# Seven block products instead of eight in twelve chunks more per layer, and attention moved into two PSUM banks

## The chip, the core and the metric

One core of a Trainium2 chip runs the whole program in one launch. The metric is device time in microseconds. TensorE (PE) multiplies, VectorE (DVE) and ScalarE (ACT) prepare operands and take results, GpSimd (POOL) and SyncE (SP) issue transfers.

## The reference

Two layers on x of 256 x 2048, all in float32:

```
h = rmsnorm(x, norm_mix[l]);  proj = h @ w_in[l]
qa, ka, va, qi, ki, wi, qb, kb, vb = split(proj)
o_a = top-k attention: 8 heads of 128; an indexer (16 heads of 64) scores all keys, the best 64 per query stay
o_b = sliding-window attention: 16 query heads, 2 key heads of 64, window 128, a sink per head
g_a, g_b = split(sigmoid(h @ w_gate[l]))
x = x + (g_a * (o_a @ w_branch_a[l]) + g_b * (o_b @ w_branch_b[l])) @ w_out[l]
x = x + relu(rmsnorm(x, norm_mlp[l]) @ w_up[l])**2 @ w_down[l]
```

and a last rmsnorm. Everything is causal in chunks of 64 positions. The key, index-weight and kb/vb columns of w_in are a first unit of their own ("misc").

## The kernel before

Every large product is cut into units of 512 output columns, and a unit into chunks of 256 rows of the weight (512 KB each). A float32 product is made of three faster ones: both operands are split into a high and a low half, and hi x hi, hi x lo and lo x hi are added. For each chunk, SP loads it into one of four buffers `raw`, ScalarE rounds it into `w_hi` (its `split`, L922), VectorE subtracts for `w_lo` (its `split`, L1350), and TensorE runs 12 matmuls of 512 columns into the two banks of a pair `acc[0]` or `acc[1]`, which alternate by unit. All engines walk the same list of chunks in the same order, each in its own queue, with semaphores between them. ScalarE may fill a slot as soon as TensorE has finished the chunk four before (`SLOTS = 4`); SP may load a buffer once the low half four before is taken.

Some chunks are "wide": the 256 x 512 block and the matching 256 x 256 of h are seen as 2 x 2 blocks and multiplied with seven block products instead of eight (`seven_products`, L532, a Winograd form). For this VectorE adds weight blocks (`weight_sums`, L1353, run before the split of the chunk ahead), the split has 7 x 256 columns instead of 4 x 256 (L929, L931 on ACT, L1371 on DVE), sums of blocks of h must exist in high and low halves (`s_hh`), and at the unit's end results in two further banks, the "sides" `wide_acc`, are added in (`add_up_sides`, L1760). Before, wide chunks are in branch B's gates (`WIDE_GATE`, chunks 1, 3, 5, 7) and in the MLP.

A layer has the misc unit, ten projection units of 8 chunks (`C_WIN`: 0 and 1 the indexer's queries, 2 and 3 qa, 4 and 5 ka, 6 and 7 va, 8 and 9 qb), then four times a branch A gate (8 chunks) and a branch product (4 chunks) from `C_MIXA`, the same for B, the out projection and the MLP. Attention is fitted between these chunks by hand: `jobs_after` (one for each engine) runs a job after a given chunk; ScalarE and VectorE come to the same list four chunks later (`AHEAD`), that is, after the split of chunk c+4 they do the part that belongs to TensorE's chunk c. Visits:

- indexer rounds at `IDX_AT` = C_WIN + 24, every fourth chunk two rounds on TensorE, top-k from `TOPK_AT` = C_WIN + 40;
- branch A, a head every second chunk from `A_AT` = C_WIN + 56: TensorE does the product with v of the head three before (`a_pv`) and the logits (`a_logits`); VectorE bias and row minimum (`a_low`), ScalarE the exponential (`a_exp`, L1020), VectorE normalises and spreads, GpSimd's transfers transpose through DRAM, and ScalarE copies the landed probabilities to `probsT` (`a_take_probsT`, L1032), one head earlier than the head whose exponential it has just done: at visit h the exponential of h, then the copy of h-2, then, at TensorE's visit h+1, its product;
- branch B, two groups of heads every fourth chunk from `B_AT` = C_MIXA + 4, in the same manner (`b_pv` two visits after `b_logits`).

Logits go to `att[0]` and `att[1]`, products with v to `att[2]`. Projections are read out by ScalarE (`take_win`, L1128) before its fourth split of the next unit, spread by VectorE (`spread_block`), and passed through DRAM by SP (`pass_on`: a store before load 7 of the unit, four fetches behind it), then placed by ScalarE.

## Time and profile before

| | us |
|---|---|
| median of 3 runs (lowest, highest) | 2659.84 (2659.27, 2660.45) |
| profiled execution | 2658.03 |
| its span | 2656.1 |
| TensorE busy, granted clock | 2641.4, 0.999 of full |

The span runs from the first to the last instruction; the time of an execution has a little more around it. A matmul's length in the trace overlaps the next one's, so costs are read as the distance from start to start. Layer 0's projections run from about 28 to 267 us, branch A's gates to about 413, branch B's after them.

### The profile page before, as it was taken

The numbers are of one execution on the slowest core, as the hardware profiler recorded it, in microseconds if no ns is written. First come the engines' busy times: TensorE is split into PE (matmuls) and PEld (weight loads), VectorE is DVE, ScalarE is ACT, GpSimd is POOL, SyncE is SP. The second block draws the span as 40 slices with busy tenths as digits, with TensorE's granted clock in tenths as the row PEclk, the third lists the DMA queues.
The fourth block names the chain that finished last, engine by engine and source line by source line (L and its number), as shares of the span: only waits on it lengthen the run. The fifth ranks groups of instructions, "written<-read, shape, count | busy, mean of one in ns | idle before, by whom it ended". The sixth has DMA issues, their size and how long they took to land.

```text
span 2656.1 us, 37301 instructions
## 1 busy us (share of the span) xinstructions
PE 2641.4 (99%) x13432; PEld 2217.1 (83%) x13432; DVE 2078.8 (78%) x3099; ACT 1448.1 (55%) x1863; POOL 215.8 (8%) x378
## 2 busy tenths in 40 slices
PE   9999999999999999999999999999999999999998
PEld 7788778888888888888888887788888888888887
DVE  5667678967898897987756766789678989989875
ACT  5445555545565655655455455555456556556554
POOL 0103110000100100100010021100000001000000
PEclk9999999999999999999999999999999999999999
DMA  7877676666775766767777666667677767667574
GB/s 260 239 236 224 222 226 195 229 231 231 244 228 191 246 216 206 240 205 232 235 237 225 224 225 221 218 202 233 227 256 231 221 208 242 209 217 234 189 248 151
DMA packets 187395, 594.52 MB, mean 224 GB/s; under 512 B 25576, under 2 KB 46612, under 8 KB 187088
## 3 DMA queue, kind: packets, MB, share of 16 engines
q1 hardware_dynamic: 166256, 536.94, 62.1%
q0 software_dynamic: 20432, 54.86, 7.5%
q8 instruction: 106, 1.74, 0.3%
q14 instruction: 73, 0.60, 0.1%
q10 hardware_dynamic: 528, 0.37, 0.1%
HBM read 544.58 MB, written 47.48 MB: 223 GB/s over the span
## 4 chain that ended last, share of the span: by engine, by line
PE 95%; DVE 3%; DMA 1%; issue 1%; ACT 0%; DVEq 0%; POOLq 0%; POOL 0%; SPq 0%; ACTq 0%
PE acc L578 24%; PE acc L579 24%; PE acc L580 24%; PE att L546 2%; PE att L548 2%; PE att L547 2%; PE acc L546 2%; PE acc L548 2%; PE acc L547 2%; PE acc L595 1%; PE acc L594 1%; PE acc L596 1%; DMA raw<-in_w_main 1%; DVE w_lo L1350 1%; DVE w_lo L1371 1%
## 5 line engine op out<-in xcount | busy, mean ns | idle before, releaser
L1350 DVE TENSOR_TENSOR w_lo<-raw,w_hi 128x1024 fp32r<-128x1024 f32 (+1 forms) x778 | 933.2, 1211 | 374.0 <-ACT w_hi L922 370.3
L922 ACT ACTIVATE w_hi<-raw 128x1024 fp32r<-128x1024 f32 (+1 forms) x778 | 813.1, 1051 | 633.5 <-PE acc L580 462.4
L578 PE MATMUL acc<-w_hi,h_hl 128*128 128x512 f32 x1848 | 735.2, 398 | 1.1 <-DVE w_lo L1350 1.1
L580 PE MATMUL acc<-w_hi,h_hl 128*128 128x512 f32 x1848 | 728.9, 394 | 0.0
L579 PE MATMUL acc<-w_lo,h_hl 128*128 128x512 f32 x1848 | 728.6, 394 | 0.0
L578 PEld LDWEIGHTS acc<-w_hi,h_hl 128*128 128x128 f32 x1848 | 347.9, 188 | 83.0 <-issue 4.9
L580 PEld LDWEIGHTS acc<-w_hi,h_hl 128*128 128x128 f32 x1848 | 347.9, 188 | 81.3
L579 PEld LDWEIGHTS acc<-w_lo,h_hl 128*128 128x128 f32 x1848 | 348.2, 188 | 76.3
L1371 DVE TENSOR_TENSOR w_lo<-raw,w_hi 128x1792 fp32r<-128x1792 f32 x166 | 335.5, 2021 | 33.5 <-ACT w_hi L931 32.4
L578 PE MATMUL acc<-w_hi,o_hl 128*128 128x512 f32 x912 | 360.4, 395 | 0.0
L579 PE MATMUL acc<-w_lo,o_hl 128*128 128x512 f32 x912 | 360.0, 395 | 0.0
L580 PE MATMUL acc<-w_hi,o_hl 128*128 128x512 f32 x912 | 359.6, 394 | 0.0
L929 ACT ACTIVATE w_hi<-raw 128x768 fp32r<-128x768 f32 x166 | 140.3, 845 | 195.0 <-PE acc L548 110.1
L931 ACT ACTIVATE w_hi<-raw 128x1024 fp32r<-128x1024 f32 x166 | 174.9, 1054 | 86.9 <-DVE raw L1365 86.7
L580 PEld LDWEIGHTS acc<-w_hi,o_hl 128*128 128x128 f32 x912 | 171.8, 188 | 40.2
L578 PEld LDWEIGHTS acc<-w_hi,o_hl 128*128 128x128 f32 x912 | 171.6, 188 | 37.7 <-issue 1.4
L579 PEld LDWEIGHTS acc<-w_lo,o_hl 128*128 128x128 f32 x912 | 171.7, 188 | 36.3
L1359 DVE TENSOR_TENSOR raw<-raw 128x512 f32<-128x512 f32 x166 | 113.3, 683 | 21.2 <-issue 11.3
L455 POOL DMA_DIRECT2D scratch<-spread x30 | 16.9, 563 | 973.2 <-DVE spread L1428 973.2
L1428 DVE STREAM_TRANSPOSE spread<-stage 128x512 f32<-128x512 f32 x112 | 73.0, 689 | 21.8 <-ACT stage L1128 17.5
L1020 ACT ACTIVATE probs<-probs,low 128x128 f32<-128x128 f32 x96 | 41.0, 428 | 85.0 <-DVE sink_d L1592 43.8
L1363 DVE TENSOR_TENSOR raw<-raw 128x256 f32<-128x256 f32 x166 | 70.6, 425 | 5.8
(298 smaller groups left out, 3614.9 us busy)
## 6 DMA issues: line engine op xcount, KB each, us to landing
raw<-in_w_main SPq DMA_DIRECT2D x928, 512.0 KB, 4.3
scratch<-spread SPq DMA_DIRECT2D x37, 512.0 KB, 2.8
moved<-scratch SPq DMA_DIRECT2D x148, 128.0 KB, 3.2
scratch<-spread POOLq DMA_DIRECT2D x30, 512.0 KB, 3.5
moved<-scratch POOLq DMA_DIRECT2D x120, 128.0 KB, 5.0
scratch_p<-spread POOLq DMA_DIRECT2D x16, 384.0 KB, 4.6
moved<-scratch_p POOLq DMA_DIRECT2D x64, 96.0 KB, 4.3
raw<-in_w_misc SPq DMA_DIRECT2D x16, 336.0 KB, 4.0
```

The lines of the kernel that those rows point to most:

```text
L546: nc.tensor.matmul(o, a_hi, hi[:, w], start=start, stop=False, skip_group_check=True)
L547: nc.tensor.matmul(o, a_hi, lo[:, w], start=False, stop=False, skip_group_check=True)
L548: return nc.tensor.matmul(o, a_lo, hi[:, w], start=False, stop=stop, skip_group_check=True)
L578: nc.tensor.matmul(o, a_hi, hi[:, kk], start=(k == 0), stop=False)
L579: nc.tensor.matmul(o, a_hi, lo[:, kk], start=False, stop=False)
L580: last = nc.tensor.matmul(o, a_lo, hi[:, kk], start=False, stop=fin)
L922: nc.scalar.activation(w_hi[s][:, 0:2 * width], raw[r][:, 0:2 * width], ACT.Copy).then_inc(hi_ready, 1)
L929: nc.scalar.activation(w_hi[s][:, 0:3 * HALF], raw[s][:, HALF:CW], ACT.Copy)
L931: nc.scalar.activation(w_hi[s][:, 3 * HALF:7 * HALF], raw[s][:, CW:2 * CW], ACT.Copy).then_inc(hi_ready, 1)
L1350: nc.vector.tensor_tensor(w_lo[s][:, 0:2 * width], raw[r][:, 0:2 * width], w_hi[s][:, 0:2 * width].bitcast(F32), ALU.subtract).then_inc(lo ...
L1359: nc.vector.tensor_tensor(r[:, 4 * HALF:6 * HALF].rearrange("p (k n) -> p k n", k=2), r[:, HALF:3 * HALF].rearrange("p (k n) -> p k n", k= ...
L1371: nc.vector.tensor_tensor(w_lo[s][:, 0:7 * HALF], raw[s][:, HALF:8 * HALF], w_hi[s][:, 0:7 * HALF].bitcast(F32), ALU.subtract).then_inc(lo ...
```

## The change

Wide chunks come to four projection units (1, 2, 6, 7) and to branch A's first two gates, chunks 1 and 5 of each: twelve a layer. The sums of h for them are made in unit 0 into `s_win`, in a part of `o_hl` that branch B fills only later; small tiles that lay in the upper half of `raw1` move there too. The sides of these units need banks, so the attention of both branches keeps to `att[0]` and `att[1]`: branch A has one logits bank and `att[1]` for the product with v, branch B puts that product in the last 128 columns of both. The indexer's visits start four chunks later, branch A's two. Read-out of a wide unit becomes: ScalarE copies a side, VectorE adds up (`add_sides_up`), ScalarE scales.

```diff
-IDX_AT, IDX_STEP, IDX_ROUNDS = C_WIN + 24, 2, 6
+IDX_AT, IDX_STEP, IDX_ROUNDS = C_WIN + 28, 2, 6
 TOPK_AT = C_WIN + 40
-A_AT, A_STEP = C_WIN + 56, 2
+A_AT, A_STEP = C_WIN + 58, 2
...
+WIN_UNITS = (1, 2, 6, 7)
+WIN_CHUNKS = (1, 5)
+A_GATES = 2
...
+        win_side_sum = win_sum_room[:, :]
...
+        s_win = o_hl[:, :, 10:14, :].rearrange("p a k s -> p a (k s)").rearrange("p a (b c) -> p a b c", b=W_SUMS)
...
+        win_sides = dict(zip(WIN_UNITS, (wide_acc[0], wide_acc[1], wide_acc[0], wide_acc[1])))
...
+                    then = {}
+                    if u - 2 in WIN_UNITS[0:2]:
+                        store, fetch = pass_on(l, E_QK + u - 2)
+                        then = {1: [store], 2: [fetch]}
+                    load_unit(l, C_WIN + 8 * u, 8, None if u - 1 in WIN_UNITS[0:2] else passing, then=then)
...
+                    pe.wait_ge(up_summed, l * LAYER_SIDES + 2)
...
-                if h >= 2:
-                    pe.wait_ge(low_ready, l * JOBS + (h - 1))
-                b = att[h % 2]
+                    pe.wait_ge(up_summed, l * LAYER_SIDES + 3)
+                else:
+                    pe.wait_ge(low_ready, l * JOBS + h)
+                b = att[0]
...
-                b, pT = att[2], probsT[h % 2]
+                b, pT = att[1], probsT[h % 2]
...
+                pe.wait_ge(low_ready, l * JOBS + (A_HEADS + min(j + 2, B_JOBS)))
                 for g in range(2):
-                    o = att[2][64 * g:64 * g + 64, :]
+                    o = [att[t][64 * g:64 * g + 64, 3 * P:4 * P] for t in range(TT)]
                     vb = misc[:, :, O_VB + 64 * g:O_VB + 64 * g + 64]
-                    nc.tensor.matmul(o[:, 0:SEQ], vb[:, 0, :], probsT[g][:, 0:SEQ], start=True, stop=False)
-                    last = nc.tensor.matmul(o[:, P:SEQ], vb[:, 1, :], probsT[g][:, SEQ:3 * P], start=False, stop=True)
+                    nc.tensor.matmul(o[0], vb[:, 0, :], probsT[g][:, 0:P], start=True, stop=True, skip_group_check=True)
+                    nc.tensor.matmul(o[1], vb[:, 0, :], probsT[g][:, P:SEQ], start=True, stop=False, skip_group_check=True)
+                    last = nc.tensor.matmul(o[1], vb[:, 1, :], probsT[g][:, SEQ:3 * P], start=False, stop=True, skip_group_check=True)
                 last.then_inc(pv_done, 1)
...
-                    unit(l * CHUNKS + (C_WIN + 8 * u), 8, h_lhs, acc[u % 2], win_between, win_before)
+                    hold = {1: [(1, misc_took, l + 1), (1, h_sums_took, l * LAYER_SUMS + 1), (5, h_sums_took, l * LAYER_SUMS + 2)],
+                            2: [(1, rows_out, 1)], 6: [(1, idx_relu, (l + 1) * IDX_ROUNDS)]}
+                    unit(l * CHUNKS + (C_WIN + 8 * u), 8, h_lhs, acc[u % 2], win_between, win_before, hold=hold.get(u, ()),
+                         wide=WIN_CHUNKS if u in WIN_UNITS else (), sum_of=win_sum, sides=win_sides.get(u))
...
+                         hold=[(1, up_summed, l * LAYER_SIDES + len(WIN_UNITS) + n)] if n < A_GATES else (),
+                         wide=WIN_CHUNKS if n < A_GATES else (), sum_of=win_sum, sides=wide_acc[1])
...
+                act.wait_ge(logits_done, l * JOBS + (A_HEADS + min(j + 3, B_JOBS)))
+                for t in range(TT):
+                    last = nc.scalar.activation(o_hl[:, 0, 8 + j, t * P:(t + 1) * P], att[t][:, 3 * P:4 * P], ACT.Copy)
+                last.then_inc(o_hi, 1)
...
+                def win_side(u):
+                    unit_done(l * CHUNKS + (C_WIN + 8 * (u + 1)))
+                    act.wait_ge(spread_ready, l * MOVES + (E_QK + min(u, 6)))
+                    nc.scalar.activation(stage[:, 0, HALF:NB], win_sides[u][0][:, HALF:NB], ACT.Copy).then_inc(sides_out, 1)
+                def win_scale(u):
+                    act.wait_ge(up_summed, l * LAYER_SIDES + WIN_UNITS.index(u) + 1)
+                    for t in range(TT):
+                        dst = stage[:, t, :] if u < 6 else va[:, t, (u - 6) * NB:(u - 5) * NB]
+                        last = nc.scalar.activation(dst, stage[:, t, :], ACT.Copy, scale=rms[:, 2 if u == 2 else 0, t:t + 1])
+                    last.then_inc(act_took, 1)
...
+                    was_wide, then = u - 1 in WIN_UNITS, {}
+                    if u == 0:
+                        then = {5: lambda: win_sums_hi(0), 7: lambda: win_sums_hi(1)}
+                    if was_wide:
+                        then[4] = lambda u=u: win_scale(u - 1)
+                    if u - 2 in WIN_UNITS[0:2]:
+                        then[0] = win_place(u - 1)
                     unit(l * CHUNKS + (C_WIN + 8 * u), 8,
-                         take=(lambda u=u: take_win(u - 1)) if u else take_misc, taken=win_place(u),
-                         jobs=win_jobs(u))
+                         take=(lambda u=u: win_side(u - 1)) if was_wide else (lambda u=u: take_win(u - 1)) if u else take_misc,
+                         taken=None if u - 1 in WIN_UNITS[0:2] else win_place(u), jobs=win_jobs(u), then=then,
+                         wide=WIN_CHUNKS if u in WIN_UNITS else (),
+                         steps=early_steps(WIN_UNITS.index(u)) if u in WIN_UNITS else None)
...
+                def early_gate_side(n):
+                    unit_done(l * CHUNKS + (C_MIXA + 12 * n + 8))
+                    act.wait_ge(dve_took, l * DVE_UNITS + n + 1)
+                    act.wait_ge(spread_ready, l * MOVES + E_M)
+                    nc.scalar.activation(stage[:, 0, HALF:NB], wide_acc[1][0][:, HALF:NB], ACT.Copy).then_inc(sides_out, 1)
+                def early_gate_tanh(n):
+                    act.wait_ge(up_summed, l * LAYER_SIDES + len(WIN_UNITS) + n + 1)
+                    for t in range(TT):
+                        last = nc.scalar.activation(stage[:, t, :], stage[:, t, :], ACT.Tanh, scale=rms[:, 1, t:t + 1])
+                    last.then_inc(act_took, 1)
...
+                    gate_then = {0: lambda n=n: early_gate_tanh(n - 1)} if 0 < n <= A_GATES else {}
...
+                for t in range(TT):
+                    s = slice(t * P, (t + 1) * P)
+                    last = nc.vector.tensor_tensor(o_hl[:, 1, 8 + j, s], att[t][:, 3 * P:4 * P],
+                                                   o_hl[:, 0, 8 + j, s].bitcast(F32), ALU.subtract)
+                last.then_inc(o_ready, 1)
...
+                def win_sums_lo(n):
+                    dve.wait_ge(h_sums_hi, l * LAYER_SUMS + n + 1)
+                    nc.vector.tensor_tensor(s_win[:, 1, n, :], sums_f, s_win[:, 0, n, :].bitcast(F32), ALU.subtract)\
+                        .then_inc(h_sums_took, 1)
+                def first_lo_second_sums():
+                    win_sums_lo(0)
+                    gate_sums(2)
...
+                def add_sides_up(g, sides, banks, i, sum_at):
+                    z, w = sides
+                    at = g * 2 + (l * LAYER_SIDES + i)
+                    steps = g * 6 + 3 * (l * LAYER_SIDES + i)
+                    quarters = stage[:].rearrange("p t (h c) -> p (t h) c", h=2)
+                    dve.wait_ge(sides_out, at + 1)
+                    nc.vector.tensor_tensor(sum_at, z[:, 0:HALF], quarters[:, 1, :], ALU.add).then_inc(up_step, 1)
+                    dve.wait_ge(up_step, steps + 1)
+                    nc.vector.tensor_tensor(quarters[:, 0::3, :], sum_at.unsqueeze(1).to_broadcast([P, 2, HALF]),
+                                            w[:].rearrange("p (h c) -> p h c", h=2), ALU.subtract).then_inc(up_step, 1)
+                    dve.wait_ge(up_step, steps + 2)
+                    nc.vector.tensor_tensor(quarters[:, 2, :], quarters[:, 3, :], w[:, 0:HALF], ALU.subtract).then_inc(up_step, 1)
+                    nc.vector.tensor_tensor(stage[:, 0, :], banks[0][:], stage[:, 0, :], ALU.add)
+                    dve.wait_ge(up_step, steps + 3)
+                    nc.vector.tensor_tensor(stage[:, 1, :], banks[1][:], stage[:, 1, :], ALU.add).then_inc(up_summed, 1)
...
+                def add_win_sides(u):
+                    add_sides_up(0, win_sides[u], acc[u % 2], WIN_UNITS.index(u), win_side_sum)
                 for u in range(N_WIN):
                     take = take_keys if u == 0 else (lambda u=u: take_stage(u - 1)) if u <= 6 or u == 9 else None
-                    unit(l * CHUNKS + (C_WIN + 8 * u), 8, take=take, jobs=lambda c, u=u: jobs_after(l, C_WIN + 8 * u + c - AHEAD))
+                    then = {}
+                    if u == 0:
+                        then = {4: lambda: gate_sums(0), 6: first_lo_second_sums}
+                    if u == 1:
+                        then = {0: lambda: win_sums_lo(1)}
+                    if u - 1 in WIN_UNITS:
+                        then[3] = lambda u=u: add_win_sides(u - 1)
+                        if u <= 6:
+                            then[5] = take
+                        take = None
+                    unit(l * CHUNKS + (C_WIN + 8 * u), 8, take=take, jobs=lambda c, u=u: jobs_after(l, C_WIN + 8 * u + c - AHEAD),
+                         then=then, wide=WIN_CHUNKS if u in WIN_UNITS else (),
+                         steps=early_steps(WIN_UNITS.index(u)) if u in WIN_UNITS else None)
...
+                         {3: lambda n=n: add_sides_up(0, wide_acc[1], acc[0], len(WIN_UNITS) + n, side_sum)} if early else ())
```

## Rows read from the trace of the kernel before

**Rows 1.** The page: busy time of the engines, and the chain that ended last.
```profile
PE 2641.4 (99%) x13432; PEld 2217.1 (83%) x13432; DVE 2078.8 (78%) x3099; ACT 1448.1 (55%) x1863; POOL 215.8 (8%) x378
...
PE 95%; DVE 3%; DMA 1%; issue 1%; ACT 0%; DVEq 0%; POOLq 0%; POOL 0%; SPq 0%; ACTq 0%
```
**Rows 2.** Windows of layer 0: stretch, length, busy time, clock, DMA share, GB/s.
```profile
28.00:100.00 72.00, 72.00 (x330) 57.30 (x330) 37.57 (x46) 35.86 (x43) 11.76 (x20) 1.00 0.84 254
...
315.00:400.00 85.00, 85.00 (x417) 65.81 (x417) 61.10 (x153) 48.79 (x100) 16.56 (x30) 1.00 0.71 223
400.00:500.00 100.00, 100.00 (x545) 86.31 (x544) 87.78 (x104) 54.20 (x60) 0.00 (x0) 1.00 0.64 207
```
**Rows 3.** Timeline of PE, branch B's first gate: start, length, line, operation.
```profile
427.18 0.39 PE L578 MATMUL acc<-w_hi,h_hl 128*128 128x512 f32 x1
...
429.96 0.28 PE L546 MATMUL att<-w_hi,s_hh 128*128 128x256 f32 x1
...
432.44 0.39 PE L578 MATMUL acc<-w_hi,h_hl 128*128 128x512 f32 x1
```
**Rows 4.** Timeline of DVE there: a wide split, weight sums, side sum.
```profile
418.96 2.02 DVE L1371 TENSOR_TENSOR w_lo<-raw,w_hi 128x1792 fp32r<-128x1792 f32 x1
420.89 0.68 DVE L1359 TENSOR_TENSOR raw<-raw 128x512 f32<-128x512 f32 x1
...
422.41 1.22 DVE L1350 TENSOR_TENSOR w_lo<-raw,w_hi 128x1024 fp32r<-128x1024 f32 x1
...
440.40 0.42 DVE L1767 TENSOR_TENSOR stage<-att,stage 128x256 f32<-128x256 f32 x1
...
443.11 0.68 DVE L1359 TENSOR_TENSOR raw<-raw 128x512 f32<-128x512 f32 x1
```
**Rows 5.** Timeline of PE, indexer scores in two halves of the array.
```profile
99.35 0.27 PE L673 MATMUL turn<-kiT_kbT,qiv 64*128 64x128 f32 x1
99.46 0.27 PE L673 MATMUL att<-kiT_kbT,qiv 64*128 64x128 f32 x1
```
**Rows 6.** The last indexer visit (chain of waits), and VectorE's splits 47 and 48.
```profile
126.86 0.43 PE acc L578
```
```profile
162.12 2.36 DVE L1350 TENSOR_TENSOR w_lo<-raw,w_hi 128x1024 fp32r<-128x1024 f32 x2
```
**Rows 7.** Timeline of PE, four visits of branch A.
```profile
206.29 0.38 PE L685 MATMUL att<-qk 128*128 128x128 f32 x2
...
212.51 0.59 PE L698 MATMUL att<-probsT,qiv 128*128 128x256 f32 x2
...
219.39 0.59 PE L698 MATMUL att<-probsT,qiv 128*128 128x256 f32 x2
...
226.27 0.59 PE L698 MATMUL att<-probsT,qiv 128*128 128x256 f32 x2
```
**Rows 8.** Timelines of DVE and ACT between them: minimum, exponential, transposed copy.
```profile
216.55 0.08 DVE L1535 DVE_READ_ACCUMULATOR2_ANT low<- 128x1 f32 x1
...
224.15 0.40 ACT L1020 ACTIVATE probs<-probs,low 128x128 f32<-128x128 f32 x1 [2.76 <-DVE low L1535]
...
225.04 0.51 ACT L1032 ACTIVATE probsT<-moved_a 128x384 f32<-128x384 f32 x1
```
**Rows 9.** Timelines of PE and ACT, branch B: visits 0, 2, 3; exponentials 1, 2; copy 1.
```profile
282.42 0.39 PE L713 MATMUL att<-kiT_kbT,qbT 64*128 64x128 f32 x2
...
306.66 0.44 PE L725 MATMUL att<-probsT,misc 128*64 128x256 f32 x2
...
319.56 0.44 PE L725 MATMUL att<-probsT,misc 128*64 128x256 f32 x2
```
```profile
298.46 0.40 ACT L1020 ACTIVATE probs<-probs,low 128x128 f32<-128x128 f32 x1 [2.67 <-DVE sink_d L1592]
...
310.89 0.40 ACT L1020 ACTIVATE probs<-probs,low 128x128 f32<-128x128 f32 x1 [2.74 <-DVE sink_d L1592]
...
315.37 0.94 ACT L1051 ACTIVATE probsT<-moved 128x384 f32<-128x384 f32 x2 [0.15 <-DMA moved<-scratch_p]
```
**Rows 10.** The page's DMA issues: count, size, median us from issue to landing.
```profile
raw<-in_w_main SPq DMA_DIRECT2D x928, 512.0 KB, 4.3
```

More of the change, by code:

```diff
@@ L97 @@
 H_SUMS = 4
+LAYER_SUMS = W_SUMS + G_SUMS + H_SUMS
 B11, B22, B21, T1, T3, T2, T4 = range(7)
@@ L655, in h_sum, with win_sum @@
                 return s_hh[:, part, pair, i * P:(i + 1) * P]
+            def win_sum(part, pair, i):
+                return s_win[:, part, pair // 2, i * P:(i + 1) * P]
             def m_lhs(part, k, t):
@@ L1170, in _ @@
                     unit(l * CHUNKS + (C_MIXA + 12 * n), 8, phase=(C_MIXA + 12 * n) % RAW, take=(lambda: take_win(9)) if n == 0 else None,
+                         wide=WIN_CHUNKS if early else (), steps=early_steps(len(WIN_UNITS) + n) if early else None,
                          taken=(lambda: place(l, E_QB + 1, qbT[:, 4:8, :])) if n == 0 else None,
                          jobs=lambda c, n=n: jobs_after(l, C_MIXA + 12 * n + c - AHEAD),
-                         then={4: lambda: gate_sums_hi(0), 6: lambda: gate_sums_hi(1)} if n == NBLK - 1 else ())
+                         then=gate_then)
@@ L1697, in take_stage, with gate_sums @@
                     spread_block(l, E_QK + u if u < 6 else E_QB + u - 8, stage)
+                def gate_sums(n):
+                    hi, lo = (h_hl[:, part, PIECES * n + 2:PIECES * n + 4, :].rearrange("p k s -> p (k s)").bitcast(F32)
+                              for part in range(2))
+                    both = stage2[:, 1, :]
+                    a11, a21, a12, a22 = (both[:, i * P:(i + 1) * P] for i in range(4))
+                    s1, s2, s3, s4 = (sums_f[:, i * P:(i + 1) * P] for i in range(4))
+                    chain.link(nc.vector.tensor_tensor(both, hi, lo, ALU.add))
+                    nc.vector.tensor_tensor(s3, a21, a11, ALU.subtract)
+                    chain.link(nc.vector.tensor_tensor(s1, a21, a22, ALU.add))
+                    chain.link(nc.vector.tensor_tensor(s2, s1, a11, ALU.subtract))
+                    nc.vector.tensor_tensor(s4, a12, s2, ALU.subtract).then_inc(h_summed, 1)
@@ L1724, in take_branch_b @@
                     spread_block(l, E_M + n, stage2)
[L1726 to L1737 removed]
                 def gate_sums_lo(n):
[L1740 removed]
+                    dve.wait_ge(h_sums_hi, l * LAYER_SUMS + W_SUMS + n + 1)
                     nc.vector.tensor_tensor(s_hh[:, 1, n, :], sums_f, s_hh[:, 0, n, :].bitcast(F32), ALU.subtract)\
@@ L1748, in _ @@
                 for n in range(NBLK):
-                    unit(l * CHUNKS + (C_MIXA + 12 * n), 8, phase=(C_MIXA + 12 * n) % RAW, take=(lambda n=n: take_branch_a(n - 1)) if n else (lambda: take_stage(9)),
+                    early = n < A_GATES
+                    unit(l * CHUNKS + (C_MIXA + 12 * n), 8, phase=(C_MIXA + 12 * n) % RAW,
+                         wide=WIN_CHUNKS if early else (), steps=early_steps(len(WIN_UNITS) + n) if early else None,
+                         take=(lambda n=n: take_branch_a(n - 1)) if n else (lambda: take_stage(9)),
                          jobs=lambda c, n=n: jobs_after(l, C_MIXA + 12 * n + c - AHEAD),
```

92 lines of the change are left out of this document (39 added, 53 removed).

## The prediction

> **What bounds the kernel now.** I read the page first: TensorE is busy 2641.4 us of a span of 2656.1, and 95% of the chain that ended last is its matmuls [rows 1]. Every microsecond taken off TensorE, or put on it as idle time, is therefore a microsecond of the kernel, if no other engine comes to hold it up. Then the windows: in the stages that change (28 to 400 us, and the same in layer 1 from about 1345) TensorE has no idle time, VectorE is busy 52 to 72%, ScalarE 50 to 57% [rows 2]. In branch B's gates, where half of the chunks already go by seven products, VectorE is at 88% and TensorE still full. Shares are averages, though, so last I read the timelines around single attention visits, since there the queues wait for each other in order. That is where I place the outcome.
>
> **What it removes.** A plain chunk is 12 matmuls of 512 columns, from 427.18 to 429.96: 2.78 us. A chunk by seven products is 21 of 256 columns, 429.96 to 432.44: 2.48 us [rows 3]. Saved: 0.30 us. Six units per layer (four projections, two gates) with two such chunks each, two layers: 24 chunks, 24 x 0.30 = **7.2 us**. Eight products of half size becoming seven would promise 0.35 us each; the small matmuls' start-to-start of 0.118 us, more than half of 0.232, takes the rest. The Trainium skill ("TensorE: Matmul & The Clock Gate", section "LDWEIGHTS (loading the stationary operand)") gives a load as its columns over 1.2 ns, 107 ns at 128. By that, 21 loads would hold a wide chunk at no less than 2.24 us; the rows at 2.48 us lie above it, and by the page the saving could be at most 0.54 us a chunk, 13 us in all, which no row reaches.
>
> **What it adds, piece by piece.**
> - *VectorE, per wide chunk:* three weight sums, 1.52 us from first start to the split behind them, and a split that starts 1.93 us before the next work instead of 1.14 [rows 4]: +2.3 us. *Per wide unit:* the side sum, 2.71 us [rows 4]. *ScalarE:* two copies (start to start 0.74 and 0.96) for one of 0.96, and a side copy of 0.28; scaling moves from before the next unit's fourth split to behind its fifth.
> - *Unit 0:* two sums of h, each like the rows of the later ones (below 3 us), beside 23 us of units with VectorE idle a third; their users come eight chunks later. Nothing.
> - *Indexer, four chunks later:* the last two rounds' additions (2.04 us each) fall on chunks 40 and 42, where VectorE now idles 1.1 to 1.7 us a chunk before chunk 44's top-k; I placed them one by one and chunk 44's start doesn't move. Then top-k at 44 to 52 meets the weight sums of 49 and 53. Today the low half of chunk 47 is ready at 163.3 and TensorE, 14 chunks of 2.78 after 126.86, wants it at 165.8 [rows 6], a margin of 2.5 us; with 2.3 us for each of the two wide chunks I get a least margin near 1 us at 53. Nothing, with up to 1 us a layer kept for the range. If the cover were gone, the 2.3 us would show in full.
> - *Transfers of units 1 and 2:* the store goes behind load 1 and the fetch behind load 2 of the unit after the next, on SP. A load queued behind them waits for the spread or the store at most about one chunk; loads land in a median 4.3 us [rows 10] and are wanted some 8 us after issue. The queue's next waiting instruction is only the load of chunk 3. On POOL nothing is added. Nothing.
> - *One logits bank in branch A:* the logits now wait for the row minimum of the head before. That is ready 3 us before the next visit today (216.6 [rows 8] against 220.0, the product with v at 219.39 and its 0.65). It falls due together with the transposed probabilities, which are later. No term of its own.
> - *Branch B's product with v:* per group two fp32 matmuls of 256 and 128 columns become three of 128, the same columns. The two groups run side by side in the array today. 12 recorded passes for 8: if hidden, nothing; if each of the four extra took its full start-to-start of 0.11 us [rows 5], 16 x 4 x 0.11 = 7 us. The nearest row is the indexer, where pairs of matmuls in two halves of the array go 0.11 us apart per pair with two loads each [rows 5], so the passes stream at their column time: 0, range to +3. The skill's load rule gives 12 loads of 64 columns 0.64 us, just the streaming time.
> - *ScalarE's copy of that product* waits for the next logits and is two instructions: about 0.7 us later, still before VectorE's split is done. Nothing.
>
> **Branch A's visits: the first stall.** Number chunks from the start of the projections. The durations below are start-to-start times of the same instructions in the timelines of 188 to 268 and 268 to 346 us, of which rows 7 to 9 are the anchors. Visits of the attention come every second chunk; TensorE's are 6.88 us apart once it also multiplies by v (212.51 to 219.39), 6.23 before [rows 7]. ScalarE hands over the transposed probabilities only behind the next head's exponential, and that waits for VectorE. Before: exponential 224.15, copy 225.04 (ready 225.55), wanted at 226.27 [rows 7, 8]. The margin is **0.7 us** there, 1.3 at other visits. Now unit 7's side sum lands on VectorE behind split 67, between heads 2 and 3. From exponential 2 to exponential 3: until the normalising starts 1.02, normalise and spread 1.29, wait for split 67's high half 0.35, split 67 1.14, side sum 2.71, then the wait until ScalarE has scaled (1.24) and copied the output (0.4) 1.76, output low half 0.34, bias and minimum 1.34: 9.95 us. Exponential 2 starts 3.83 us after TensorE's visit 2 (or 4.6, if unit 6's side sum and chunk 61's weight sums leave 0.8 us behind), and the copy is ready 1.38 us after exponential 3. So ready 15.2 to 16.0 us after visit 2; TensorE wants it after 6.23 + 6.88 = 13.1. **Stall 2.1 to 2.9, taken as 2.5 us per layer.** Behind it a step of VectorE takes 6.3 to 6.6 against 6.88, the margin grows again, and unit 8's spread at chunk 75 uses it up without a stall by my sum (margin 0.4).
>
> **Gate 1 in branch B's visits: the second.** Visits come every four chunks. Count from visit 0 (282.42 before) [rows 9]. New: gate 0's side sum behind split 91 and the weight sums of 93 before split 92: 10.5 (start of split 91) + 1.14 + 2.71 + 1.52 + 1.14 + 1.48 = 18.5 for exponential 1, where it was 16.0 (298.46) [rows 9]. Then 1.77 + 0.74 + 0.96 + 0.96 + 0.93 for copy 0 gives 23.9, exactly when visit 2 wants it (306.66 less 282.42, less 0.3 for wide chunk 85): no stall, no margin left of 2.6 us. To exponential 2: 1.89 + 1.27 + 0.45 wait + 1.93 (wide 93) + 0.95 spread + 1.14 + 1.20 (branch product) + 1.14 + 1.52 and 0.2 wait (weight sums of 97) + 1.14 + 0.5 + 1.48 = 14.8, where it was 12.43; so 33.3. The copy is ready 5.36 later at 38.7; visit 3 wants it at 319.56 - 282.42 - 0.6 = 36.5. **Stall 2.2 us per layer**, 0.5 to 3.5. After 97 there is no wide chunk; gate 2 gives the time back to VectorE.
>
> **Sum.** -7.2 + 2 x (2.5 + 2.2) = +2.2 us. The profiled execution took 2658.03, 1.8 below the median of 2659.84, its span 1.9 less; so 2660.2 for it, and **2662.0** on the median.
>
> **Rivals.** The measurement tells 0.2% (5.3 us) from nothing.
> 1. *The cover holds.* If both stalls together stay under 1.0 us a layer, the kernel gains over 5.3 us: about 2654. For: VectorE idles a quarter to a half of these stages, and branch B's gates stand more. Against: there no attention waits in the same queues, and 0.7 us is the measured margin.
> 2. *The loads are dragged in: slower.* A load of chunk c is issued when the low half of c-4 is taken. While VectorE is behind, it reaches the weight sums of c after two splits (2.3 us), but the load takes a median 4.3 us to land [rows 10]: up to 2 us more for each wide chunk met in that state, 93 and 97, perhaps 53 and 61. It decides from 1.6 us more per layer (5.3 - 2.2, over 2); with 2 us at two chunks, 2 x 4 more on 2662, 2670. For: a queue behind its time pays for each load in full. Against: in branch B's gates every second chunk asks for its load that early, and TensorE stays full [rows 2].
> 3. *The small passes cost,* 3 us or more in 16 calls: 2665, on the edge.
> 4. *A slip of mine in one stall only:* 2657 to 2660, no difference.
>
> **How the numbers follow.** Forecast with case 4 (no difference): 0.52. Cover holds, faster: 0.22. Loads, or passes on top of both stalls, slower: 0.26. The range reaches to the cover case at 2654 and most of the way to the load case, 2668; the likeliest case's own is 2657 to 2665.
>
> **What would show it.** L546 to L548 with 24 x 7 more instructions each at 0.28 us; TensorE's idle time before a product with v in unit 8, ended by ScalarE's copy (2 to 3 us, once a layer), and again before the second product of branch B (about 2 us). VectorE's busy time up by 24 x 2.3 + 12 x 2.7 = 88 us less overlap. I'm wrong if these waits are missing or under 1 us; if they are over 4; if waits stand before the indexer or in chunks 49 to 61; or if branch B's product takes over 1 us where it takes 0.81.

## The result, and the profile after

| | before | after |
|---|---|---|
| median (lowest, highest), us | 2659.84 (2657.35, 2661.04) | 2685.92 (2682.10, 2691.00) |
| span of the profiled execution | 2656.1 | 2684.0 |
| granted clock of it | 0.999 | 0.996 |

Five runs each; the ratio is 1.0102 with a 95% interval of 1.0089 to 1.0114. The kernel is 1% slower. The forecast was 2662.0, its range 2654 to 2668: the time lies 18 us above the range.

The page of the kernel after; the first line answers to the first of [rows 1]:
```profile
PE 2650.3 (99%) x13712; PEld 2233.7 (83%) x13712; DVE 2170.4 (81%) x3271; ACT 1468.2 (55%) x1919; POOL 215.8 (8%) x378
```
280 matmuls more: 24 chunks x 9, and 64 for branch B's product with v, so the change does what it says. A new wide chunk takes 2.49 us (75.22 to 77.71), as forecast. VectorE has 91.6 us more (forecast 88). Idle time of TensorE (the span less its busy time) went from 14.7 to 33.7 us. What its weight loads waited for, over the whole span (line after the change, releaser, us in all, times, longest):
```profile
PEld att L692 <- ACT stage L1041: 8.6, 4, 3.7
PEld att L746 <- ACT probsT L1078: 8.2, 9, 1.9
PEld acc L593 <- DVE w_lo L1426: 6.7, 11, 2.8
PEld att L718 <- ACT probsT L1059: 6.6, 3, 3.1
```
The second and the fourth are the two stalls of the forecast: branch B's product with v, and branch A's. The first (the indexer's scores) and the longest wait of the third (2.8 us, a weight split) stand where the forecast costed the change at nothing. A weight load runs ahead of its matmul, so this view says more than TensorE lost: its matmuls idle 7.0, 4.3, 4.1 and 5.8 us at these four lines. Windows of layer 0, against [rows 2]:
```profile
75.00:100.00 25.00, 22.67 (x118) 19.00 (x117) 13.96 (x18) 11.01 (x13) 4.55 (x8) 1.00 0.72 212
100.00:103.00 3.00, 3.00 (x10) 2.31 (x10) 2.93 (x5) 1.38 (x2) 0.60 (x1) 0.60 0.79 229
...
130.00:146.00 16.00, 12.67 (x61) 9.29 (x59) 10.64 (x19) 7.29 (x10) 2.98 (x5) 0.97 0.91 271
146.00:148.00 2.00, 2.00 (x5) 1.61 (x6) 1.97 (x3) 1.33 (x3) 0.00 (x0) 0.50 0.15 21
...
212.00:240.00 28.00, 25.32 (x121) 20.96 (x121) 22.53 (x58) 14.51 (x31) 9.08 (x17) 0.95 0.64 204
...
310.00:340.00 30.00, 28.56 (x167) 23.50 (x166) 24.43 (x69) 16.43 (x40) 4.41 (x8) 1.00 0.59 192
```
Read the second number (TensorE busy) against the first, then the clock, third from the right: 2.3 us idle before 100, 3.3 before 146, 2.7 before 236; behind each the clock is low for some microseconds, while the 1.4 us idle in the last window cost no clock. The timelines say who is late. ScalarE from 86 us on, then TensorE at the two waits and at the forecast ones:
```profile
86.37 1.06 ACT L949 ACTIVATE w_hi<-raw 128x1024 fp32r<-128x1024 f32 x1 [1.74 <-PE acc L595]
96.15 1.06 ACT L1011 ACTIVATE qiv<-moved 128x1024 f32<-128x1024 f32 x1 [8.72 <-DMA moved<-scratch]
97.12 1.99 ACT L949 ACTIVATE w_hi<-raw 128x1024 fp32r<-128x1024 f32 x2
...
121.22 1.06 ACT L1011 ACTIVATE qk<-moved 128x1024 f32<-128x1024 f32 x1 [7.62 <-DMA moved<-scratch]
...
142.32 1.06 ACT L1011 ACTIVATE qk<-moved 128x1024 f32<-128x1024 f32 x1 [6.73 <-DMA moved<-scratch]
143.28 0.58 ACT L1041 ACTIVATE stage<-att 128x512 f32<-128x512 f32 x1
```
```profile
99.47 0.51 PE L593 MATMUL acc<-w_hi,h_hl 128*128 128x512 f32 x1 [2.33 <-DVE w_lo L1426]
...
144.40 0.48 PE L692 MATMUL att<-kiT_kbT,qiv 64*128 64x256 f32 x1 [3.33 <-ACT stage L1041]
...
235.82 0.70 PE L718 MATMUL att<-probsT,qiv 128*128 128x256 f32 x2 [2.68 <-ACT probsT L1059]
...
333.06 0.43 PE L746 MATMUL att<-probsT,misc 128*64 128x128 f32 x2 [1.44 <-ACT probsT L1078]
```
ScalarE stands 8.72 us before it places unit 1's turned block; the unit's next weight splits stand behind that copy. When it goes on, VectorE's low halves are late in turn, and TensorE waits 2.33 us at 99.47. The same happens at 121 with unit 2's block. At 142 it is unit 3's block, whose placing the change didn't move; it is late because VectorE spread it late (131.68), behind indexer scores that had waited for the read-outs behind the placing at 121. The indexer's next read-out (L1041) stands behind it, and TensorE waits for that at 144.40. VectorE before unit 3's spread:
```profile
123.28 0.29 DVE L1581 TENSOR_SCALAR score<-stage,misc 128x128 f32<-128x128 f32 x1 [8.43 <-ACT stage L1041]
...
131.68 1.30 DVE L1504 STREAM_TRANSPOSE spread<-stage 128x512 f32<-128x512 f32 x2
```
The way of unit 1's block to ScalarE, on VectorE and on SP's queue:
```profile
81.02 2.02 DVE L1447 TENSOR_TENSOR w_lo<-raw,w_hi 128x1792 fp32r<-128x1792 f32 x1 [0.43 <-ACT w_hi L958]
82.96 1.30 DVE L1504 STREAM_TRANSPOSE spread<-stage 128x512 f32<-128x512 f32 x2
```
```profile
84.28 0.33 SPq L353 DMA_DIRECT2D scratch<-spread  x1
85.39 0.33 SPq L337 DMA_DIRECT2D raw<-in_w_main  x1
90.73 2.79 SPq L359 DMA_DIRECT2D moved<-scratch  x4
```
The spread starts at 82.96, the store at 84.28, the fetch at 90.73, the placing at 96.15. From the spread to a block that has landed it is 13.2 us, more than four chunks of 2.78 us. The Trainium skill ("DMA: Bandwidth & Descriptors", section "Anatomy of one DMA — SWDGE (gpsimd) path") gives a transfer a fixed part of about 2 us and bytes over 436 GB/s, an estimate of 3.2 us for 512 KB, by a fit that is for another path than this queue. The profile's page has a median of 2.9 us for these stores on SP; this one, between weight loads, took 6.4, and the fetch behind it was issued 6.45 us after it.

Branch B's product with v, after; it answers to the visit at 306.66 of [rows 9]:
```profile
318.67 0.43 PE L746 MATMUL att<-probsT,misc 128*64 128x128 f32 x2
318.94 0.27 PE L747 MATMUL att<-probsT,misc 128*64 128x128 f32 x1
...
319.43 0.38 PE L748 MATMUL att<-probsT,misc 128*64 128x128 f32 x2
319.74 0.50 PE L733 MATMUL att<-kiT_kbT,qbT 64*128 64x128 f32 x4
```
From its first matmul to the next logits it takes 1.07 us, where it took 0.81 before. 16 of these make 4.2 us.

**The account.** The span is 27.9 us longer. The terms:

- saved by the chunks: -7.2 us;
- small passes: +4.2;
- idle time: +19.0;
- before each of 29 waits (the 27 of the view above and two at wide chunks) the last matmul counts as busy for its length of 0.39 us instead of the step of 0.23: 0.16 x 29 = +4.6, an estimate from lengths;
- low clock behind four waits (99, 144, 236 and 1564 us), each 1.7 us by windows of 2 us (0.79, 0.50, 0.86 behind the first: 2 x (0.21 + 0.50 + 0.14)): +6.8.

The sum is 27.4.

### The profile page after: what moved, and what is told of

It reads as the page before. It is cut to its first block, busy times and chain, and to the rows that moved or that the text cites. A ratio compares the mean times of both kernels' runs of the same rounds, so it can differ in the third digit from the quotient of the medians.

```text
span 2684.0 us, 38123 instructions
## 1 busy us (share of the span) xinstructions
PE 2650.3 (99%) x13712; PEld 2233.7 (83%) x13712; DVE 2170.4 (81%) x3271; ACT 1468.2 (55%) x1919; POOL 215.8 (8%) x378
## 4 chain that ended last, share of the span: by engine, by line
PE 79%; DVE 10%; DMA 5%; ACT 3%; issue 3%; SPq 0%; POOL 0%; POOLq 0%; ACTq 0%; DVEq 0%
PE acc L593 19%; PE acc L594 19%; PE acc L595 19%; DVE w_lo L1426 3%; PE att L561 2%; PE att L563 2%; PE att L562 2%; PE acc L561 2%; PE acc L563 2%; PE acc L562 2%; DMA scratch<-spread 1%; PE acc L610 1%; PE acc L609 1%; PE acc L611 1%; DMA raw<-in_w_main 1%
## 5 line engine op out<-in xcount | busy, mean ns | idle before, releaser
L1426 DVE TENSOR_TENSOR w_lo<-raw,w_hi 128x1024 fp32r<-128x1024 f32 (+1 forms) x754 | 902.4, 1209 | 283.2 <-ACT w_hi L949 281.2
L949 ACT ACTIVATE w_hi<-raw 128x1024 fp32r<-128x1024 f32 (+1 forms) x754 | 782.7, 1049 | 527.3 <-PE acc L595 362.2
L593 PE MATMUL acc<-w_hi,h_hl 128*128 128x512 f32 x1752 | 699.4, 399 | 3.7 <-DVE w_lo L1426 3.6
L595 PE MATMUL acc<-w_hi,h_hl 128*128 128x512 f32 x1752 | 693.0, 396 | 0.0
L594 PE MATMUL acc<-w_lo,h_hl 128*128 128x512 f32 x1752 | 692.7, 395 | 0.0
L1447 DVE TENSOR_TENSOR w_lo<-raw,w_hi 128x1792 fp32r<-128x1792 f32 x190 | 384.0, 2021 | 51.8 <-ACT w_hi L958 50.8
L593 PEld LDWEIGHTS acc<-w_hi,h_hl 128*128 128x128 f32 x1752 | 331.2, 189 | 81.8 <-DVE w_lo L1426 6.3
L595 PEld LDWEIGHTS acc<-w_hi,h_hl 128*128 128x128 f32 x1752 | 330.9, 189 | 77.8
L594 PEld LDWEIGHTS acc<-w_lo,h_hl 128*128 128x128 f32 x1752 | 331.5, 189 | 71.7
L956 ACT ACTIVATE w_hi<-raw 128x768 fp32r<-128x768 f32 x190 | 160.6, 845 | 210.7 <-PE acc L563 120.2
L958 ACT ACTIVATE w_hi<-raw 128x1024 fp32r<-128x1024 f32 x190 | 200.0, 1053 | 93.9 <-DVE raw L1441 93.5
L1435 DVE TENSOR_TENSOR raw<-raw 128x512 f32<-128x512 f32 x190 | 129.7, 683 | 19.0 <-DMA raw<-in_w_main 13.2
L1439 DVE TENSOR_TENSOR raw<-raw 128x256 f32<-128x256 f32 x190 | 80.8, 425 | 6.6
L1441 DVE TENSOR_TENSOR raw<-raw 128x256 f32<-128x256 f32 x190 | 80.8, 425 | 6.5
```

The source lines that it names most:

```text
L593: nc.tensor.matmul(o, a_hi, hi[:, kk], start=(k == 0), stop=False)
L594: nc.tensor.matmul(o, a_hi, lo[:, kk], start=False, stop=False)
L595: last = nc.tensor.matmul(o, a_lo, hi[:, kk], start=False, stop=fin)
L949: nc.scalar.activation(w_hi[s][:, 0:2 * width], raw[r][:, 0:2 * width], ACT.Copy).then_inc(hi_ready, 1)
L956: nc.scalar.activation(w_hi[s][:, 0:3 * HALF], raw[s][:, HALF:CW], ACT.Copy)
L958: nc.scalar.activation(w_hi[s][:, 3 * HALF:7 * HALF], raw[s][:, CW:2 * CW], ACT.Copy).then_inc(hi_ready, 1)
```

## The experiments

Each ran beside the kernel before on the same chip, in four groups: e1 to e4, e5 to e8, e9 to e12, e13 and e14. Medians are in us; ratios to that kernel have their 95% interval. The last column is the median less that of the kernel before in the same group; for the kernel after it is +26.1. The ratio is not quite the quotient of the two medians; it differs from it by up to 0.0007. That kernel's median moves between the groups from 2658.21 to 2660.45, so runs of different groups are compared by this column. The intervals are 2.4 us either way for 11 runs, 3.2 to 3.7 for 5 or 6, and wider for a difference of two such runs.

| run | median | ratio | before | over before |
|---|---|---|---|---|
| e1_banks | 2661.69 | 1.0012 (1.0003, 1.0021) | 2658.21 | +3.5 |
| e2_late | 2675.84 | 1.0059 (1.0045, 1.0072) | 2658.21 | +17.6 |
| e3_late_idx | 2672.13 | 1.0048 (1.0035, 1.0062) | 2658.21 | +13.9 |
| e4_no7 | 2679.15 | 1.0072 (1.0058, 1.0086) | 2658.21 | +20.9 |
| e5_no_gates | 2679.52 | 1.0076 (1.0062, 1.0089) | 2658.38 | +21.1 |
| e6_no_gates_old_pv | 2676.19 | 1.0072 (1.0058, 1.0086) | 2658.38 | +17.8 |
| e7_all_moved | 2658.17 | 1.0001 (0.9992, 1.0010) | 2658.38 | -0.2 |
| e8_moved_old_pv | 2655.24 | 0.9987 (0.9978, 0.9996) | 2658.38 | -3.1 |
| e9_stall_short | 2659.57 | 1.0004 (0.9995, 1.0013) | 2658.78 | +0.8 |
| e10_stall_long | 2660.08 | 1.0004 (0.9995, 1.0013) | 2658.78 | +1.3 |
| e11_moved_unit7 | 2666.17 | 1.0029 (1.0017, 1.0041) | 2658.78 | +7.4 |
| e12_moved_gate1 | 2662.68 | 1.0014 (1.0005, 1.0023) | 2658.78 | +3.9 |
| e13_stall_mid | 2666.01 | 1.0019 (1.0010, 1.0028) | 2660.45 | +5.6 |
| e14_stall_big | 2672.17 | 1.0042 (1.0028, 1.0056) | 2660.45 | +11.7 |

### e1_banks: the banks alone

The kernel before with nothing but the attention of both branches in two banks: the hunks of `a_logits`, `a_pv`, `b_pv` and their read-outs, no wide chunk.
```diff
-                b = att[h % 2]
+                b = att[0]
...
-                    o = att[2][64 * g:64 * g + 64, :]
+                    o = [att[t][64 * g:64 * g + 64, 3 * P:4 * P] for t in range(TT)]
```


> The kernel before with one part of the change alone: both branches' attention in two banks (one logits bank in branch A, branch B's product with v in six passes a group instead of four), visits where they were, no new wide chunk. Queue theory (the loss comes from waits of VectorE and ScalarE in the attention's queues): within 0.1% of before, 2658 to 2662, no wait of TensorE for logits. Rival, small passes: 16 calls at 0.2 to 0.45 us more each, 2663 to 2667. Rival, the single logits bank: TensorE waits for the row minimum in branch A.

Measured: +3.5 us in the medians (0.8 to 5.6 by the ratio's interval). Its trace has no wait for the row minimum or the transposed probabilities. So the single logits bank causes no wait, and the small passes cost something near the 4.2 us of the timeline.

### e2_late and e3_late_idx: who waits for the landed block

Placing two splits later; then also the indexer's rounds two chunks earlier, so that its read-outs don't stand behind the placing.
```diff
-                        then[0] = win_place(u - 1)
+                        then[2] = win_place(u - 1)
...
-IDX_AT, IDX_STEP, IDX_ROUNDS = C_WIN + 28, 2, 6
+IDX_AT, IDX_STEP, IDX_ROUNDS = C_WIN + 26, 2, 6
```


> The changed kernel with ScalarE's placing of units 1 and 2's blocks two chunks later in its queue (behind split 2 of the next unit instead of split 0). Placing theory (ScalarE stands up to 8.7 us in front of a block that hasn't landed, and with it every high half behind it): the waits before unit 3's chunks (2.8 and 1.2 us) and the clock lost behind the first (about 1.8 us) go, so 5 to 6 us less than the changed kernel, near 2680; the wait in front of the fourth indexer round stays. Rival, VectorE's side sums in units 2 and 3 are what is late: no change.

> As the run before it, and the indexer's visits start two chunks earlier (C_WIN + 26), so that the take of round 3 no longer stands behind the placing of unit 3's block in ScalarE's queue. Placing theory: the four waits of TensorE for an indexer take (1.1, 3.7, 1.1, 2.7 us) and one clock step of 1.8 go too; together 14 to 16 us less than the changed kernel, near 2671. Rival, VectorE's load in units 3 to 5 decides: the waits move and stay, less than 5 us gained.

Measured: 17.6 over the kernel before, 8.5 less than the kernel after (expected 5 to 6 less), and 13.9 over, 3.7 less again and 12.2 less in all (expected 14 to 16). The 3.7 alone is within the noise of two medians of five runs; the traces carry it. Timeline of ScalarE in e2:
```profile
96.43 1.06 ACT L1011 ACTIVATE qiv<-moved 128x1024 f32<-128x1024 f32 x1 [3.67 <-DMA moved<-scratch]
```
and windows of e3, stretches where the kernel after lost the most:
```profile
75.00:100.00 25.00, 25.00 (x129) 21.16 (x128) 18.09 (x22) 12.96 (x16) 4.10 (x8) 1.00 0.88 260
100.00:130.00 30.00, 30.00 (x160) 24.01 (x159) 23.80 (x41) 17.68 (x23) 4.76 (x8) 1.00 0.90 247
130.00:160.00 30.00, 30.00 (x138) 23.97 (x137) 21.50 (x62) 13.59 (x16) 4.17 (x7) 1.00 0.85 223
```
The block comes at the same time (96.43 against 96.15), but ScalarE has done two splits in between and waits only 3.67 us, and TensorE has no idle time there. The indexer's waits (L692) shrink from 8.6 to 2.2 us of weight loads with the placing alone, because the blocks behind come earlier too: unit 3's is placed at 135.19, where it was 142.32. In e3 the rest of them is gone, and TensorE is full to 160 us. The placing is the cause, not VectorE's added work, all of which is still there. The indexer's step without the placing's was not run, so what it is worth by itself is open.

### e4_no7: unit 7 plain
```diff
-WIN_UNITS = (1, 2, 6, 7)
+WIN_UNITS = (1, 2, 6)
```


> The changed kernel without unit 7's wide chunks and side sum (units 1, 2, 6 and the two gates stay). Queue theory: the wait of 3.1 us in front of a product with v in each layer goes, and the clock lost behind it (1.4 and 1.8 us); four chunks cost 0.3 us more each: 2 x 3.1 + 3.2 - 1.2 = 8 us less, near 2678. Rival, the single logits bank or the visits two chunks later cause that wait: it stays, and the kernel is 1.2 us slower.

Measured: 20.9 over the kernel before, 5.1 less than the kernel after, where 8 were expected; at five runs each the two can't be told apart. The waits before branch A's product with v are gone in both layers. The profile has one indexer wait of 5.1 us, where the longest in the kernel after is 3.7; why is open. e11 measures unit 7's stall with those waits away.

### e5_no_gates and e6_no_gates_old_pv: branch B's visits and passes
```diff
-A_GATES = 2
+A_GATES = 0
```
e6 besides takes `b_pv`, `b_o_hi` and `b_o_lo` from the kernel before.

> The changed kernel, but branch A's first two gates by plain chunks (the four projection units stay by seven products). Visit theory (the second stall is gate 0's side sum and the weight sums of gate 1's wide chunks between branch B's visits): TensorE's waits for ScalarE's transposed probabilities in branch B, 8.2 us over both layers in the changed kernel, vanish; 8 wide chunks become plain, 8 x 0.30 = 2.4 us given back; so about 5.8 us below the changed kernel, 2680. Rival (branch B's attention itself is slower because its small product comes in three passes, its copy and its low half in two pieces): the waits stay at more than half, 4 us or more, and the time stays at 2684 to 2688.

> As the run without wide gates, and besides branch B's product with v, its copy and its low half as in the kernel before (third bank, two passes of 256 and 128 columns per group); possible because no wide chunk uses that bank during branch B any more. Small-pass theory (each of the 16 products with v takes 0.26 us longer in three passes): 4.2 us below the run without wide gates, about 2676; the product with v takes 0.81 us again from its first matmul to the chunk behind it. Rival (the added microseconds are in the waits, not in the passes): no difference from that run beyond 1.5 us.

Measured: 21.1 over the kernel before, 4.9 less than the kernel after (expected 5.8), with no wait left for the transposed probabilities in branch B; and 17.8 over, 3.3 less again (expected 4.2). In e6 the product takes 0.81 us again (314.11 to 314.92). e6's runs reach from 2669.54 to 2682.82, so the two medians can't carry the 3.3 alone; it takes e1, e7 and e8 beside them.

### e7_all_moved and e8_moved_old_pv: everything together
```diff
-IDX_AT, IDX_STEP, IDX_ROUNDS = C_WIN + 28, 2, 6
+IDX_AT, IDX_STEP, IDX_ROUNDS = C_WIN + 26, 2, 6
...
-WIN_UNITS = (1, 2, 6, 7)
+WIN_UNITS = (1, 2, 6)
...
-A_GATES = 2
+A_GATES = 1
...
-                        then[0] = win_place(u - 1)
+                        then[2] = win_place(u - 1)
```
e8 has `A_GATES = 0` and branch B's product with v as before.

> The changed kernel with four things moved or left out together: ScalarE's placing of units 1 and 2's blocks two splits later, the indexer's rounds two chunks earlier, unit 7 plain, gate 1 of branch A plain. If the changed kernel's loss is the waits that the single edits took away one by one, and they add up: 16 wide chunks save 16 x 0.30 = 4.8 us, the product with v in three passes costs 4.2, about 1 us is left in small waits for weight splits, so 2659 to 2661, no difference from the kernel before; granted clock 0.999 or more. If a stall that is taken away only comes back at the next wait (VectorE or ScalarE have too much work in all): above 2667.

> As the run with four things moved, but with both gates plain and branch B's product with v as in the kernel before: 12 wide chunks (units 1, 2 and 6). Saved 12 x 0.30 = 3.6 us, no longer 4.2 us for small passes: 2656 to 2658, so 1.5 to 3.5 us below the kernel before, and 2 to 4 below the run with four things moved. If the small passes cost nothing, it is 1.2 us above that run instead (four wide chunks fewer).

Measured: 2658.17 and 2655.24 (11 runs each). The stalls are gone together and none came back elsewhere; what remains in e7 is the saving of 4.8 against the passes' 4.2. e8 is 2.9 below e7 with four wide chunks (1.2 us) fewer, which puts the passes at 4.1 us, with some 3.4 either way. e8 is 3.1 below the kernel before, where its 12 wide chunks should save 3.6. It is the only version that is clearly below, by 0.13% (0.04 to 0.22).

### e11_moved_unit7 and e12_moved_gate1: each stall on clean ground

e7 with `WIN_UNITS = (1, 2, 6, 7)`, and e7 with `A_GATES = 2`.

> The run with all moved, with unit 7's two chunks by seven products again. Visit theory for branch A: the wait of 3.1 us before one product with v per layer is back, 6.2 us, with 1.8 us of clock behind each; four wide chunks save 1.2 us: 8.6 us above that run, 2667 (2664 to 2668). Rival (the wait in the changed kernel came down from the indexer's and the placing's delays, which are gone here): under 1 us of wait, no difference or 1 us faster.

> The run with all moved, with branch A's gate 1 by seven products again (and gate 0). Visit theory for branch B: TensorE's waits for the transposed probabilities in branch B are back, 7 to 8 us over both layers, mostly under 2 us each and so without loss of clock; four wide chunks save 1.2 us: 6 to 7 us above that run, 2664 to 2665. Rival (the waits belong to gate 0's side sum alone, which that run has too): no difference, 0 to 1.2 us faster.

Measured: 7.4 and 3.9 over the kernel before, which is 7.6 and 4.1 more than e7 (expected 8.6, and 6 to 7). With the 1.2 us that the four chunks save, unit 7's stall costs 8.8 us (4.4 a layer) and gate 1's 5.3 (2.7 a layer), with some 4 and 3.4 us either way. Weight loads' waits of e11, then of e12:
```profile
PEld att L718 <- ACT probsT L1059: 6.3, 2, 3.1
```
```profile
PEld att L746 <- ACT probsT L1078: 6.0, 4, 2.3
```
Both are there with the placing and the indexer out of the way: they belong to the visits. TensorE itself idles 2.70 and 2.69 us in e11, with a low clock at each, and 0.97, 1.89 and 1.44 in e12, with a low clock behind the 1.89.

### e9_stall_short, e10_stall_long, e13_stall_mid, e14_stall_big: a stall by itself

The kernel before, with one copy of ScalarE cut into small ones at heads 3 and 6 of branch A; 16, 22, 36 and 48 pieces. Of the first:
```diff
+                if h in (3, 6):
+                    cuts = [(slice(k, k + 1), slice(i, i + 1), s) for k in range(3) for i in range(QUARTERS)
+                            for s in ((slice(0, 16), slice(16, 32)) if 3 * i + k < 4 else (slice(0, 32),))]
+                for k, i, s in cuts:
+                    last = nc.scalar.activation(dst[:, k, i, s], src[:, k, i, s], ACT.Copy)
```


> The kernel before, with ScalarE's copy of the transposed probabilities of branch A's heads 3 and 6 cut into 16 small copies (same data, same result), so that TensorE comes to wait for it at 4 places in all. A small copy takes an estimated 0.2 us from start to start (by the 0.19 us of the accumulator reads, the nearest row), so 16 take 2.8 us more than the one of 0.41; less a margin of 0.7 to 1.3 us, TensorE idles 1.5 to 2.1 us four times, 6 to 8.5 us. Clock theory (an idle time of 3 us or more pulls the granted clock to 0.50 for some 3.6 us afterwards, which costs 1.8 us on top; one of 2.7 or less costs nothing but itself): the time grows by the idle time alone, the granted clock of the windows behind the stalls stays at 1.00. Rival (every stall costs clock in proportion): the time grows by more than the idle time and the clock behind each stall falls.

> As the run with short stalls, but 22 small copies at the same four places: 1.2 to 1.5 us more each, so TensorE idles 2.9 to 3.6 us four times. Clock theory: the granted clock falls to about 0.50 behind each of the stalls of 3 us or more, and the time grows over the kernel before by the idle time and 1.8 us for each of them, up to 7 us beyond the idle time. Rival (the low clock seen behind long stalls in the changed kernel has another cause, such as the sort of matmuls there): the time grows by the idle time alone.

These two told nothing of the clock: a piece takes 0.11 us from start to start, not 0.2 (22 pieces in 2.44 us), so weight loads wait 0.4 us twice in e9 and 1.0 or less twice in e10, and TensorE itself idles not at all in e9 and 0.54 us twice in e10. Their times differ from the kernel before by less than can be told.

> The kernel before, with the copy of the transposed probabilities of branch A's heads 3 and 6 cut into 36 small copies at 0.11 us from start to start (measured in the run with 22): 3.9 us for 0.41, less a margin of 1.0 us, so TensorE idles up to 2.5 us at four places, 8 to 10 us in all. Clock theory (a wait of about 3 us brings the granted clock down to 0.50 for a while, one below 2.7 does not): the time grows by the sum of the waits, no clock below 1.00 behind them. Rival (each wait costs clock in proportion): more than the waits.

> As the run with 36 small copies, but 48: 5.2 us for 0.41, TensorE idles up to 3.8 us at four places, 13 to 15 us in all. Clock theory: the granted clock falls to about 0.50 behind each wait of 3 us or more and the time grows by the waits and about 1.8 us for each such fall, up to 7 us more, 2679 for the sum of both. Rival (the low clock in the changed kernel has another cause): the time grows by the waits alone, 2672 to 2674.

Timeline of TensorE in e13, and windows of e13 around it:
```profile
1555.92 0.70 PE L698 MATMUL att<-probsT,qiv 128*128 128x256 f32 x2 [1.83 <-ACT probsT L1039]
```
```profile
1552.00:1556.00 4.00, 2.17 (x10) 1.42 (x9) 1.29 (x4) 4.00 (x39) 1.05 (x2) 1.00 0.57 195
1556.00:1560.00 4.00, 4.00 (x14) 3.33 (x15) 3.16 (x5) 2.02 (x3) 2.19 (x4) 0.65 0.36 49
```
and the same of e14:
```profile
1558.37 1.22 PE L698 MATMUL att<-probsT,qiv 128*128 128x256 f32 x2 [2.94 <-ACT probsT L1039]
```
```profile
1556.00:1560.00 4.00, 1.63 (x5) 1.45 (x6) 0.70 (x1) 4.00 (x26) 1.21 (x4) 0.70 0.12 49
1560.00:1564.00 4.00, 4.00 (x12) 3.23 (x11) 3.17 (x10) 1.24 (x5) 1.09 (x2) 0.50 0.67 193
```
In e13 the long waits are two, not four (one a layer), and in e14 too: they stand at head 3, and the copies at head 6 mostly hide (0.4 us of idle time in e14, none in e13). The times grow by 5.6 and 11.7 us. For e14 that is 3.3 us of idle time a layer, and the low clock behind the long waits: 1.7 us in layer 0, about 3 in layer 1, together 11.3. Its 2672.17 lies where the rival put it, at 2672 to 2674, but by luck: the rival's sum has four long waits and no low clock, the trace two and a low clock behind both. A wait with nothing else of the change beside it can bring the low clock: the rival of another cause falls. The half of the clock theory that set a limit at 2.7 us falls too: in e13 an idle time of 1.83 us did it, in both layers.

The other way round, e3 has the stall of branch A's product with v in both layers (2.71 and 2.72 us) and no low clock behind either. Its first, and the window behind it:
```profile
227.59 0.70 PE L718 MATMUL att<-probsT,qiv 128*128 128x256 f32 x2 [2.71 <-ACT probsT L1059]
```
```profile
228.00:232.00 4.00, 4.00 (x21) 3.38 (x20) 3.96 (x8) 1.70 (x3) 1.04 (x2) 1.00 0.42 150
```
So such a stall can cost clock and need not.

## Why the prediction was wrong

- **The failed step: "Transfers of units 1 and 2", costed at "Nothing".** It asked what the moved store and fetch do to the loads behind them on SP, and answered that well enough. It didn't ask what stands behind the instruction that waits for the fetch: ScalarE's placing, put after the first split of the unit after the next. The spread had become late (side sum, weight sums and a wide split ahead of it), the round trip took 13.2 us from there, and ScalarE stood 8.7 and 7.6 us before the two moved blocks, then 6.7 before unit 3's. Moving the placing alone gave back 8.5 us of 26.1.
- **"Indexer, four chunks later", "Nothing".** Only VectorE's additions and top-k were placed, with a margin near 1 us. The loss was on ScalarE: read-outs behind the placing, 8.6 us of waits at L692. Most of that followed from the step above and went with it (2.2 left in e2); the rounds moved by two chunks took the rest, 3.7 us beyond e2.
- **First stall, 2.5 us a layer: mechanism, place and length right, price too low.** TensorE idles 2.68 and 2.69 us (forecast 2.1 to 2.9; the 3.1 of the view is the weight load's). The cost is 4.4 a layer (e11 against e7), because a low clock of about 1.7 us followed each.
- **Second stall, 2.2 us a layer, range 0.5 to 3.5: right.** TensorE idles 4.3 us over both layers, 2.2 a layer. The largest part, 1.44 and 1.45 us, stands before the second product, at visit 3 as forecast, the rest before its neighbours. Cost 2.7 (e12 against e7). Both stalls together are 10.1 us of idle time, where the forecast has 9.4.
- **Branch B's product with v, taken as 0, range to +3.** 4.2 us by the timeline, 4.1 by e8 against e7: outside its own range. The reading of the nearest row (the indexer's pairs stream at their column time) didn't carry over; the measured cost lies between it and the bound of 7 us from the full start-to-start. Rival 3 was real, as an addition.
- **ScalarE's later copy in branch B, nothing; one logits bank, no term:** right; e1 has no wait for either.
- **Saving, 7.2 us:** borne out. The new wide chunks take 2.49 us, and e7 and e8 stand within 1 us of where their 16 and 12 chunks put them.
- **No term for the clock.** Behind four waits of the profiled execution it was low, which cost 6.8 us. The sum took a stall as worth its own length.
- Rival 2 (loads dragged in) didn't show: VectorE's weight sums wait for a load not once from 275 to 345 us, and once, 0.4 us, in the same stretch of layer 1 (1600 to 1670). The slow case came, by another mechanism than the one it was given to.

With the terms as measured, -7.2 + 4.2 + 2 x (4.4 + 2.7) gives 11.2 us over the kernel before. e3, which lacks only the missed waits of placing and indexer, lies 13.9 over it (9.3 to 16.5 by its interval), so the terms account for it within the noise. The missed waits are the other 12.2 of the 26.1 us.

## What to carry to other kernels

When a step is moved to later, follow the block to the last engine that waits for it, and list what that engine's queue holds behind the wait; the queue that issues the transfer is only half of the question. Where nearly all time is one full engine, put an instruction that waits for a transfer where the block has landed by the traced round trip, counted from the engine that now delivers late. Price a stall of TensorE at its length and, for the lengths that brought a low clock here (1.8 us and more), at the risk of a slow stretch behind it: the 4.4 us of unit 7's stall are what fifteen wide chunks save at 0.3 us each.

## What the runs showed of the hardware

- The granted clock around idle times of TensorE, in all traces, from 20 us to its last matmul. At idle times of 1.8 us or more (the longest 4.68) it went to 0.50 of full, 1.2 GHz, in 22 of 30 cases; at 1.4 to 1.7 us in none of 11. The eight exceptions are 2.29 us in the kernel after, 2.71 and 2.72 in e3, 3.08 in e4, 2.00 in e5, and 2.72, 2.03 and 2.67 in e6. Four idle times of 1.91 to 1.94 us, all 9 us from the start (before, e8, e13, e14), brought no fall either.
- Length alone doesn't decide it: the same wait before branch A's product with v, 2.67 to 2.72 us in every trace that has it, came with the low clock in 8 of 12 cases (both layers in the kernel after, e2, e5 and e11, neither in e3 and e6). What decides is open. A fall costs 1.7 us in most cases, in three (e2, e4, e14) 2 to 3.
- The Trainium skill ("TensorE: Matmul & The Clock Gate", section "What's actually happening") names two levels for the gate, 1.2 and 2.4 GHz. The windows agree: none is below 0.50, and values between are stretches with both.
- Kernels with such waits spread more: e6 reaches over 13.3 us in 5 executions, e8, without them, over 4.4 in 11. Part of it can be the clock: the profiled execution of e3, with no fall, is the shortest of its five, 5.2 us below their median.
- Branch B's product with v as three fp32 matmuls of 128 columns a group instead of one of 256 and one of 128, two groups side by side in the array, took 1.07 us where it took 0.81, though the columns are the same.
- Small copies of ScalarE (16 columns) follow each other every 0.11 us (22 in 2.44 us in e10), though each is recorded with 0.20.
